# Expert loop on TensorE: the down projection of one expert pair set directly before the up projection of the next

## What is computed

```python
def step(out, args):
    tok, g, e = args
    xe = xpad[tok]
    h = jax.nn.silu(xe @ w1[e]) * (xe @ w3[e])
    y = (h @ w2[e]) * g[:, None].astype(xe.dtype)
    return out.at[tok].add(y), None
```

## Time and profile before

| | |
|---|---|
| median of three runs | 1522.33 us (1522.10 to 1525.82) |
| profiled execution, its own time | 1529.43 us |
| its span, first to last instruction | 1527.6 us |
| mean granted TensorE clock | 0.971 |
| TensorE matmuls busy | 1449.1 us, 95% |
| VectorE (DVE) busy | 508.8 us, 33% |
| ScalarE (ACT) busy | 356.5 us, 23% |
| HBM read | 459.52 MB, 301 GB/s over the span |

### The profile page before, as it was taken

The page is one execution under the profiler, slowest core; times in us unless marked ns, Lnnn a source line. Parts: engine busy times, 40 slices in busy tenths (PEclk is TensorE's granted clock), DMA queues, the critical chain, the costliest instruction groups (busy, mean ns, idle before and its releaser), DMA issues.

```text
span 1527.6 us, 22033 instructions
## 1 busy us (share of the span) xinstructions
PE 1449.1 (95%) x8704; PEld 912.2 (60%) x8704; DVE 508.8 (33%) x840; ACT 356.5 (23%) x878; POOL 49.6 (3%) x75
## 2 busy tenths in 40 slices
PE   7978999999999999999999999999998999999987
PEld 3467586565566656654487567666665665666543
DVE  0387351332223323232611236232332322232253
ACT  1127132222122212221210332222221221222211
POOL 1210010000000000000100001000000000000000
PEclk9979999999999999999999999999999999999989
DMA  9530238999989989998564404599998999999951
GB/s 305 171 148 1 92 157 356 407 411 401 407 358 413 406 354 403 409 410 334 180 220 154 177 1 165 211 406 420 404 409 352 391 418 377 375 406 413 419 204 55
DMA packets 80801, 462.05 MB, mean 302 GB/s; under 512 B 9152, under 2 KB 9376, under 8 KB 30528
## 3 DMA queue, kind: packets, MB, share of 16 engines
q1 hardware_dynamic: 78112, 452.07, 74.0%
q0 software_dynamic: 2592, 8.53, 1.7%
HBM read 459.52 MB, written 1.05 MB: 301 GB/s over the span
## 4 chain that ended last, share of the span: by engine, by line
PE 90%; DVE 5%; ACT 2%; issue 2%; DMA 1%; SPq 0%; DVEq 0%
PE ps L886 30%; PE ps L914 15%; PE ps L856 9%; PE ps L928 8%; PE ps L614 4%; PE ps L773 4%; PE ps L1033 4%; PE ps L728 3%; PE ps L745 2%; PE ps L797 2%; PE ps L586 1%; PE ps L896 1%; PE ps L713 1%; PE ps L806 1%; PE ps L868 1%
## 5 line engine op out<-in xcount | busy, mean ns | idle before, releaser
L1661 DVE TENSOR_TENSOR o_tok<-ps,o_tok 128x1024 f32<-128x1024 f32 x128 | 156.7, 1224 | 345.5 <-PE ps L928 345.5
L886 PE MATMUL ps<-ring,proj 128*64 128x256 f32 x2048 | 239.0, 393 | 15.2 <-issue 15.2
L914 PE MATMUL ps<-ring,qkT 128*64 128x512 f32 x1024 | 233.8, 598 | 1.2 <-ACT qkT L1208 1.2
L886 PEld LDWEIGHTS ps<-ring,proj 128*64 128x64 f32 x2048 | 150.4, 142 | 101.0 <-issue 35.8
L914 PEld LDWEIGHTS ps<-ring,qkT 128*64 128x64 f32 x1024 | 68.2, 136 | 133.3 <-issue 133.3
L1653 DVE SCALAR_TENSOR_TENSOR roped<-roped,rows,ps 128x256 f32<-128x256 f32 x64 | 30.8, 481 | 342.5 <-ACT roped L1202 342.5
L1229 ACT ACTIVATE y_hi<-ps 128x1024 fp32r<-128x1024 f32 x64 | 65.5, 1023 | 293.3 <-PE ps L928 287.4
L886 PE MATMUL ps<-ring,pT 128*64 128x256 f32 x1024 | 123.1, 382 | 2.2 <-ACT gb_row L1196 2.2
L886 PE MATMUL ps<-ring,gb_row 128*64 128x256 f32 x1024 | 121.5, 379 | 0.0
L856 PE MATMUL ps<-sel,x_hi 128*128 128x512 f32 x256 | 118.3, 462 | 0.0
L928 PE MATMUL ps<-y_hi,selT 128*128 128x512 f32 x256 | 111.6, 436 | 4.0 <-DVE y_lo L1667 4.0
(11 more groups left out here) (248 smaller groups left out, 1409.9 us busy)
## 6 DMA issues: line engine op xcount, KB each, us to landing
ring<-in_exp_w_dram SPq DMA_DIRECT2D x384, 1024.0 KB, 10.8
ring<-in_od_w_in_dram SPq DMA_DIRECT2D x6, 2048.0 KB, 8.2
ring<-in_ev_w_in_dram SPq DMA_DIRECT2D x4, 2048.0 KB, 18.5
ring<-in_ple_w_gate_dram SPq DMA_DIRECT2D x4, 2048.0 KB, 11.4
ring<-in_sh_w_dram SPq DMA_DIRECT2D x6, 1024.0 KB, 7.2
ring<-in_ev_w_o_dram SPq DMA_DIRECT2D x2, 2048.0 KB, 11.9
ring<-in_od_w_o_dram SPq DMA_DIRECT2D x2, 2048.0 KB, 8.9
gb_row<-in_ln_g_dram POOLq DMA_DIRECT2D x4, 512.0 KB, 9.3
```

The lines of the kernel that those rows point to most:

```text
L886: ins = pe.matmul(ps[b * SLOTS:(b + 1) * SLOTS, 2, w * FE:(w + 1) * FE], xe(odd, c)[:, u * P + b * SLOTS:u * P + (b + 1) * SLOTS], views[b ...
L914: ins = pe.matmul(ps[b * SLOTS:(b + 1) * SLOTS, 4 + half, :], hT[:, f, b * SLOTS:(b + 1) * SLOTS], views[b][:, f, half * PIECE:(half + 1) ...
L1661: dve.tensor_tensor(y_acc[:, t, :], ps[:, bank:bank + 2, :].rearrange("p b n -> p (b n)"), y_acc[:, t, :], ALU.add)\
```

## The change

In each pair's step, half 0 of the scatter stands directly behind up, ahead of the gather; half 1 of the scatter and the one-hot transposes stand behind the transposes of h, ahead of down. Down is the step's last piece. The code of the other engines is the same.

```diff
@@ -941,17 +941,17 @@
                     exp_up(m, o, odd, u, par, first and M0 == 0)
+                    if scatter_last:
+                        scatter(m - 1, 0, 1 - par, M0 == 0 and isinstance(m, int) and m == 1)
                     if gather_next:
                         pe.wait_ge(sem("xe_copied"), 4 * o + (4 * O0 + 4 + u))
                         gather(o + 1, u)
                     h_transpose(m)
                     if scatter_last:
-                        scatter(m - 1, 0, 1 - par, M0 == 0 and isinstance(m, int) and m == 1)
-                    exp_down(m, par, first and M0 == 0)
+                        scatter(m - 1, 1, 1 - par, False)
                     if selT_next:
                         sel_transpose(m + 1, o + 1 if u == 3 else o, (u + 1) % 4)
-                    if scatter_last:
-                        scatter(m - 1, 1, 1 - par, False)
+                    exp_down(m, par, first and M0 == 0)
```

## The result

The changed kernel takes 1529.66 us (median of 11 runs, 1525.70 to 1534.34) against 1523.85 us before (11 runs, 1514.75 to 1528.56). The ratio is 1.0042, with a 95% interval of 1.0023 to 1.0061: 6.4 us slower, or 0.4%. The forecast was slower by 20.6 us.

What follows compares the result with a forecast made beforehand. TensorE, busy 95% of the span, was taken to bound the kernel. The terms summed to +20.6 us on the profiled 1529.43, giving 1550.0; less 7.1 to the median, 1542.9 us, 1.4% slower, range 1530 to 1562.

Steps and rivals of the forecast that it cites:

- Part 1: Between down and the next up, two fewer changes of tile width per step: 0.23 us at 62 places, -14.3 us.
- Part 2: The gather no longer follows up, so its first matmul's weights load ahead: 0.2 us in 54 steps, -10.8 us.
- Part 3: At u == 3, scatter half 1 waits for DVE's add, delayed by the one-hot matrix: 12 stalls of 2.54 us, +30.5 us.
- Rival A: Borders save 0.6 us a step and the clock holds 2.4 GHz, outweighing the stall: faster, 1512.8 us; chance 0.04.
- Part 4: TensorE's clock falls to half speed after each of the 12 stalls, 1.5 us each, +18 us.
- Rival B: The stall at u == 3 comes but the clock stays up in it: +2.6 us, 1524.9 us; chance 0.08.
- C: Rival: after each stall the clock falls as long as behind the jumps, 2.7 us lost each: 1557.3 us; chance 0.20.
- Part 5: At the loop's four jumps back, scatter, one-hot and down run in the idle time: 1.2 us less each, -4.8 us.
- Part 6: Last octet, no gather: the 1.0 us idle for h goes, a 1.2 to 1.3 us add wait comes, +2 us.
- Part 7: Costed at nothing: one-hot transposes' wait for the copy of hT, the split of y, SP's load queue, the DMA.
- rival D: Between stalls the DMA becomes the bound, so the border and gather gains never come: +45.7 us, 1568.0 us; chance 0.04.

## Why the prediction was off

**Part 1, two changes of width (-14.3 us): right.** Two of them added to the changed kernel cost 0.23 us a step. The row's value stands against the full tail of a matmul, 0.34 a step.

**Part 2, the gather (-10.8): right.** 0.24 instead of 0.47 us for its first matmul, 0.34 instead of 0.31 behind the first scatter matmul. Parts 1 and 2 together were to make a plain step 0.43 us shorter; it is 0.44.

**Part 3, the new wait (+30.5): right in mechanism, place and number.** 12 stalls. In octet 0 the step grows by 2.56 us, as reckoned; in the loop by 2.7, so 32 us. Rival A, which needed no fall of the clock and 0.52 us a step, is out.

**Part 4, the clock behind the stall (+18): the mechanism right, the number of falls too high.** I took all 12 stalls to be followed by a low clock, from two rows of the kernel before. It is 7 of 12 with the loop written out, at 1.6 to 1.7 us each, so 11 to 12 us. (In the changed kernel itself the stall of pair 15 in layer 1 was followed by 6.8 us of it, which cost 3.0 us, in both traces.) The price of one was right (1.5). Rival B (none) and C (2.7 us each) are out.

**Part 5, the jumps (-4.8): the step that failed.** I wrote that "the jump can't begin its work before the scatter's wait is met", and let scatter, one-hot and down run beside it. The jump's idle time in layer 1 is 2.99 and 3.36 us where it was 3.44 and 3.44: 1.2 us each were to go, and 0.45 and 0.08 did. The premise quoted held; what failed is what I made of it. I had held fixed the 6.85 us from the end of the add (405.80) to up. It is 7.96 now (410.50 to 418.46), since the branch comes later after the wait: before, it stood directly behind scatter half 1 and started 0.15 us after the add's end; now one-hot and down stand ahead of it, and it starts 1.4 us after. So the matmuls that run beside the branch are 3.3 us of its 6.2 before and 3.5 of its 6.0 now, nearly the same.

What changed is another thing, of which the prediction had no term: in layer 2 nothing was fetched at the jump at all. The kernel before pays 22.5 us for its jumps (written out: 0.9852), the changed one 1.0042 / 0.9985 = 1.0057, 8.7 us. So the change takes 14 us from them, where I had 4.8. Of the 14.2 us by which the forecast was too high, this is 9 and the clock of part 4 is 6; the other parts miss by 1 or 2 us. I had also counted their idle time alone; the low clock behind each (2.6 us and more in the earlier trace rows) goes with it. The piece of the forecast that doesn't touch the jumps, +25.4 us, measured +20.6.

**Part 6, the last octet (+2): right, a little too high.** The waits are 0.94 us where 1.00 was, and I had 1.2 to 1.3. The step is 14.29 against 14.35 us. Part 1 has already taken 0.23 off these steps, so the share of part 6 is +0.17 a step where I had 0.25.

**Part 7 and rival D.** No new wait for the split of y or a load appeared in the changed kernel. The one-hot transposes do wait for the copy of h, 0.9 us in all, but only in pair 0 of each layer, where no scatter covers it; down waited there before, 1.2 us. Rival D rested on 410 GB/s as a limit; 421 were reached.

The account for the changed kernel on medians: parts 1 and 2, -24 to -25; stalls +32; clock +12; jumps -14; last octets -0.4; together +5 to +6, measured +6.4.

What stays open: why the jumps of layer 2 were free in all three traces of the changed kernel and of the one with the add first, and not in those of the kernel before (one of two free in the second trace). The loop has the same length and place in the program in both. That down stands last can't be the whole cause: with down in two pieces half of it stands last too, and both jumps of layer 2 cost time. The packets of q8 show one thing that goes with the cost. At each of the six jumps of layer 2 that took time, in four traces, one more packet starts 0.3 to 1.7 us ahead of the fetch for the jump (before: 1155.6 and 1156.2 us); at the free ones there is neither. This fits a next piece, behind the loop's end, that is asked for just before the jump and pushes out the first one, and the order of the last instructions ahead of the jump may decide it. That cause is argued and not shown; no run changed this order alone.

## What to carry to other kernels

Before a wait is moved up, look at what its releaser's engine has to do first: here a wait of 2.4 us came where none had shown, because the add stood behind other work on DVE that waited for the same engine, and one exchange of lines turned +0.4% into -2.3%. A loss that recurs at each jump back of a loop may hang on where the loop's instructions lie, so price it by writing the loop out before an explanation is built on it. An engine's saved time is worth what the next limit leaves: once the stalls were gone, fewer waits on TensorE in the last octet bought nothing, since the loads' lead had been used up.

## What the runs showed of the hardware that I had not expected

- A jump back on TensorE costs nothing if no piece of the loop is fetched at it: its branch took 0.2 us. Where a fetch came the branch took 5.8 to 7.6 us, of which 1.0 to 5.0 us were idle time, by how long the matmuls ahead of it still ran; in most cases a low clock stood in or behind it. Which it is can differ between two executions of one program (the kernel before: 81 and 72 packets on q8). The Trainium skill (Runtime: NRT & Kernel Launch, Instruction fetch mechanics) says that a taken branch whose target isn't in the current window of two pages forces a fetch before execution goes on; the traces agree where the fetch came, 4 times in the first trace of the kernel before. They don't agree on two pages: the free jumps go back over a round of the loop that takes some nine packets where it is fetched (81 less 63, for two rounds).
- The same idle time of 2.4 us was followed by a granted clock of 0.5 in 7 cases and by 1.00 in 5, in one program. It cost 1.6 to 1.7 us where it came. With the loop written out, too, it came behind pairs 7, 15 and 23 of each layer and not behind 11 and 19; why is open.
- A busy share of the DMA of 1.00 was no limit: 410 GB/s before and 421 GB/s in the fastest kernel, both with a share of 1.00 to 1.01.
- 160 empty instructions with a semaphore increment at the start of TensorE's program took 0.15 us each and delayed its first matmul from 4.45 us, where it had waited for a load, to 25.4 us.
